# Issuing the two matmuls of a k tile in turn instead of in pairs of two

## The chip, the cores and the metric

The kernel runs on one core of a Trainium2 chip. The metric is the device time of one execution in microseconds (us).

## The reference, cut to what matters

One layer of a hybrid encoder on 256 tokens of width 2048 in f32: a norm, an input projection to a Mamba-2 scan and to a sliding-window attention, an output projection with a residual, and then a retrieval of single-neuron experts (PEER). The change lies in the first product of that retrieval. In the reference it is a gather:

```python
def block(args):
    xb, ib, gb = args
    u = jnp.take(u_tab, ib, axis=0)
    act = jax.nn.gelu(jnp.einsum("thkd,td->thk", u, xb), approximate=False)
    v = jnp.take(v_tab, ib, axis=0)
    return jnp.einsum("thk,thkd->td", gb * act, v)
```

`u_tab` and `v_tab` hold 16384 experts of 2048 numbers; each token picks 128 of them (8 heads, 16 each).

## The kernel before

The kernel doesn't gather from `u_tab`. It computes the product of all 16384 rows with all 256 tokens densely, in 128 chunks of 128 experts (chunks `C_U` to `C_U + 127`), and later uses the values that the routing asks for. Then comes the dense product with `v_tab`.

**The split of a product.** TensorE multiplies numbers rounded to a shorter mantissa (`float32r`). To keep f32 accuracy, weights and activations are both cut into a high and a low part, and a product is high x high + high x low + low x high. For a chunk the raw weights come by DMA into `raw` (four slots of 1024 columns, two per chunk), ScalarE rounds them into `high`, VectorE writes the difference into `low`; `lo_done` counts the halves that are ready, `used` those that TensorE has finished with. The activations lie in `acts`, for each k tile first the 256 columns of the high part, then the 256 of the low part: `hi_tile(k)` is the first, `lo_tile(k)` the second, `both_tiles(k)` the 512 columns of both.

**An ordinary product** (`product`, input projection, output projection and queries) has 16 k tiles, and for each of them three matmuls of 256 columns into one accumulator: high weights x high part, high weights x low part, low weights x high part.

**A product of the expert stage** (`paired=True`, the 128 chunks of `u_tab`) has two matmuls for each k tile. The wide one multiplies the high weights by the 512 columns of both parts into a whole PSUM bank, `ps[:, par, :]`. The narrow one multiplies the low weights by the 256 columns of the high part into the first half of the same bank, `ps[:, par, 0:T]`. Each matmul is preceded by a load of its 128 x 128 weights. ScalarE copies the second half of the bank to SBUF (L865), VectorE adds the first half to it (L1481), ScalarE applies Gelu (L870, L874). Two banks alternate. `paired_product` issues these matmuls: for each two k tiles first the two wide ones (L1739), then the two narrow ones (L1743). It waits for `lo_done` ahead of each half chunk, and in the first chunk for a few counts of `tile_lo` (the dictionary `READY_AT`), while the activations are still being cut.

**The rest of the expert work.** The chunks are issued by a hardware loop of two chunks per turn. Beside them VectorE works out the routing, GpSimd scatters the gates, and SyncE issues the loads. After the last chunk TensorE goes on with `v_tab` (`expert_rows`), where all matmuls are 512 columns wide and successive ones write different PSUM banks (L2102, L2104, L2114, L2116, L2118); its first matmul waits for the weights that VectorE writes from the last product (L1647).

Of the kernel before, what the change touches and what calls it, by code (L numbers as in the profile page):

```python
# [22 lines left out]
P = 128  # L23
T = 256
D = 2048
KT = D // P
# [33 lines left out]
PIECE = 1024  # L60
# [49 lines left out]
def build(nc, x_t, small, id_iota, w_in, w_out, w_q, keys, u_tab, v_tab, g_f, out):  # L110
# [8 lines left out]
    with ExitStack() as ctx:  # L119
        def sb(stack, name, cols, dt=F32):  # L120
            return stack.enter_context(nc.sbuf_tensor(name, [P, cols], dt))

        def sem(name):
            return ctx.enter_context(nc.semaphore(name))

        raw = sb(ctx, "raw", RING * PIECE)
        high = sb(ctx, "high", RING * PIECE, F32R)
        low = sb(ctx, "low", RING * PIECE, F32R)
# [32 lines left out]
        ps = ctx.enter_context(nc.psum_tensor("ps", [P, 8, 512], F32))  # L161
# [90 lines left out]
        hi_tile = lambda k: acts[:, ds(2 * T * k, T)]  # L252
        lo_tile = lambda k: acts[:, ds(2 * T * k + T, T)]
        both_tiles = lambda k: acts[:, ds(2 * T * k, 2 * T)]
# [44 lines left out]
        lo_done = sem("lo_done")  # L299
        used = sem("used")  # L300
# [9 lines left out]
        tile_lo = sem("tile_lo")  # L310
# [1411 lines left out]
        def _(pe):  # L1722
            mm = nc.tensor.matmul

            READY_AT = {0: 8, 8: 14, 14: 15, 15: 16}

            def paired_product(c, par, acc, ready):

                both = ps[:, par, :]
                tile_of = lambda t, s, k: t[:, s * PIECE + k * P:s * PIECE + (k + 1) * P]  # L1730
                for half in range(2):
                    s = 2 * par + half
                    pe.wait_ge(lo_done, 2 * c + half + 1)
                    for two in range(0, 8, 2):
                        for k in (two, two + 1):
                            kk = 8 * half + k
                            if ready is not None and kk in READY_AT:
                                pe.wait_ge(tile_lo, ready + READY_AT[kk])
                            mm(both, tile_of(high, s, k), both_tiles(kk), start=(kk == 0), stop=False,  # L1739
                               skip_group_check=True)  # L1740
                        for k in (two, two + 1):
                            kk = 8 * half + k
                            ins = mm(acc, tile_of(low, s, k), hi_tile(kk), start=False, stop=(kk == KT - 1),  # L1743
                                     skip_group_check=True)
                    ins.then_inc(used, 1)

            def product(c, par, midway=None, ins_hi=None, ins_lo=None, ready=None, late=None,
                        paired=False):

                early = isinstance(c, int) and c in early_bank  # L1750
                if not early:
                    pe.wait_ge(taken, c - 1)
                acc = ps[:, early_bank[c] if early else par, 0:T]
                src_hi, src_lo = (hi_tile, lo_tile) if ins_hi is None else (ins_hi, ins_lo)
                if paired:
                    paired_product(c, par, acc, ready)
                    return
                for half in range(2):
                    s = 2 * par + half
                    pe.wait_ge(lo_done, 2 * c + half + 1)  # L1760
                    for k in range(8):
                        kk = 8 * half + k
                        if ready is not None and kk in READY_AT:
                            pe.wait_ge(tile_lo, ready + READY_AT[kk])
                        if kk == KT - 2 and late:
                            late()
                        a_hi, a_lo = src_hi(kk), src_lo(kk)
                        wh = high[:, s * PIECE + k * P:s * PIECE + (k + 1) * P]
                        wl = low[:, s * PIECE + k * P:s * PIECE + (k + 1) * P]
                        mm(acc, wh, a_hi, start=(kk == 0), stop=False)  # L1770
                        mm(acc, wh, a_lo, start=False, stop=False)  # L1771
                        ins = mm(acc, wl, a_hi, start=False, stop=(kk == KT - 1))  # L1772
                    ins.then_inc(used, 1)
                    if midway and half == 0:
                        midway()
# [86 lines left out]
            first_half(0, 1)  # L1862
            first_half(1, 1)
            product(2, 0)
            product(3, 1, sum_x)
            product(4, 0)
            turn_dt()
            product(5, 1)
# [108 lines left out]
            for s in range(SSD_TILES - 1):  # L1977
                c = C_Q + 1 + s
                acc = ps[:, c % 2, 0:T]
# [95 lines left out]
            for k in range(KT):  # L2075
                ins = nc.tensor.transpose(ps[0:SPARSE, 4 + k // 4, k % 4 * P:(k % 4 + 1) * P],
                                          h_sb[:, k * T + DENSE:(k + 1) * T], ident)
# [18 lines left out]
            def narrow_rows(par, hf, start=False, stop=False):  # L2096

                vh, vl = table_piece(par, hf)
                w = w_t[par]
                acc = [ps[:, 4 + 2 * hf + n, :] for n in range(2)]  # L2100
                for n in range(2):
                    mm(acc[n], w[:, DENSE:DENSE + 2 * SPARSE], vh[n], start=start, stop=False, skip_group_check=True)  # L2102
                for n in range(2):
                    ins = mm(acc[n], w[:, DENSE:DENSE + 2 * SPARSE], vl[n], start=False, stop=stop, skip_group_check=True)  # L2104
                return ins
# [64 lines left out]
            for hf in range(2):  # L2170
                pe.wait_ge(lo_done, 2 * (C_END - 2) + hf + 1)
                ins = narrow_rows(before, hf)
# [88 lines left out]
```

## Time and profile before

| | |
|---|---|
| median of 3 runs | 1730.2 us (1730.1 to 1730.77) |
| the profiled execution | 1730.2 us, span 1728.4 us |
| mean granted TensorE clock | 0.997 of full speed |
| TensorE busy | 1712.3 us, 99% of the span |
| weight loads busy | 1507.2 us, 87% |
| VectorE busy | 1326.5 us, 77% |
| ScalarE busy | 920.3 us, 53% |
| stage of the change | 416.7 to 1130.6 us |

The span runs from the first to the last instruction on the core; the execution's own time adds what lies around it. PE is TensorE's matmuls, PEld its weight loads, DVE is VectorE, ACT ScalarE, POOL GpSimd, SP SyncE. Durations of matmuls overlap, since they are pipelined and their ends are modelled: how fast TensorE works is seen in the distances of the starts.

### The profile page before, as it was taken

Reading aid. Unit: us, or ns where it says so; the run is one execution under the profiler, and the core shown is the slowest. Engines: PE = TensorE matmul, PEld = TensorE weight load, DVE = VectorE, ACT = ScalarE, POOL = GpSimd, SP = SyncE. Lnnn points to the kernel's source line nnn. Section 1 sums busy time; section 2 is a strip of 40 time slices with the busy share of each in tenths; the row PEclk is TensorE's granted clock in tenths of the full one; section 3 lists DMA queues with packets and bytes.
Section 4 is the critical chain, followed back from the end, with each engine's and each line's share of the span. In section 5 each row is a group of like instructions: output and inputs, shape, how many; then the busy total and the mean of one; then the engine's idle time right before and its main releaser. Section 6 shows DMA issues by size and latency. Waiting matters only on the chain.

```text
span 1728.4 us, 27916 instructions
## 1 busy us (share of the span) xinstructions
PE 1712.3 (99%) x10171; PEld 1507.2 (87%) x10171; DVE 1326.5 (77%) x2178; ACT 920.3 (53%) x1567; POOL 542.7 (31%) x336
## 2 busy tenths in 40 slices
PE   9999999999999999999999999999999999999997
PEld 8999999999888888888888888888888888888885
DVE  7878878767999999555555666668878888888887
ACT  6545655444554555544444444455555555555556
POOL 0000000000007787877783000058545422222210
PEclk9999999999999999999999999999999999999999
DMA  7654568776657888877787888898999999999994
GB/s 259 217 195 163 172 190 278 225 237 207 202 192 194 191 194 202 199 190 199 196 192 203 265 264 266 263 365 334 361 342 362 360 360 354 366 363 358 367 333 139
DMA packets 186549, 445.79 MB, mean 258 GB/s; under 512 B 59360, under 2 KB 94448, under 8 KB 177904
## 3 DMA queue, kind: packets, MB, share of 16 engines
q1 hardware_dynamic: 146976, 373.47, 64.1%
q0 software_dynamic: 39504, 71.55, 15.6%
q8 instruction: 25, 0.41, 0.1%
q14 instruction: 44, 0.36, 0.1%
HBM read 423.79 MB, written 20.57 MB: 257 GB/s over the span
## 4 chain that ended last, share of the span: by engine, by line
PE 99%; DMA 0%; DVE 0%; ACT 0%; DVEq 0%; SPq 0%; issue 0%
PE ps L1739 28%; PE ps L1743 14%; PE ps L2118 7%; PE ps L2114 7%; PE ps L2116 7%; PE ps L2102 7%; PE ps L2104 7%; PE ps L1770 4%; PE ps L1771 4%; PE ps L1772 4%; PE ps L1953 3%; PE ps L1954 3%; PE ps L1955 3%; PE ps L2067 0%; DMA raw<-w_in 0%; PE ps L1941 0%
## 5 line engine op out<-in xcount | busy, mean ns | idle before, releaser
L1739 PE MATMUL ps<-acts,high 128*128 128x512 f32 x2048 | 643.5, 395 | 0.0
L960 DVE TENSOR_TENSOR low<-raw,high 128x1024 fp32r<-128x1024 f32 x378 | 460.2, 1222 | 87.3 <-ACT high L644 78.1
L1743 PEld LDWEIGHTS ps<-acts,low 128*128 128x128 f32 x2048 | 384.7, 188 | 91.0
L644 ACT ACTIVATE high<-raw 128x1024 fp32r<-128x1024 f32 x378 | 395.3, 1051 | 85.8 <-PE ps L1772 37.8
L1743 PE MATMUL ps<-acts,low 128*128 128x256 f32 x2048 | 402.3, 278 | 0.0
L1739 PEld LDWEIGHTS ps<-acts,high 128*128 128x128 f32 x2048 | 311.7, 189 | 0.3 <-DVE low L960 0.2
L637 ACT ACTIVATE high<-raw 128x1024 fp32r<-128x1024 f32 x172 | 182.6, 1062 | 171.4 <-PE ps L2118 169.5
L598 POOL DMA_INDIRECT big<-v_tab,half_sb x64 | 119.5, 1868 | 480.1 <-DVE big L1641 287.0
L967 DVE TENSOR_TENSOR low<-raw,high 128x1024 fp32r<-128x1024 f32 x172 | 206.4, 1221 | 64.6 <-ACT high L637 64.4
L578 POOL DMA_INDIRECT gate_scratch<-gates_sb,cells_sb x128 | 208.3, 1627 | 69.5 <-issue 69.5
L865 ACT ACTIVATE side<-ps 128x256 f32<-128x256 f32 x128 | 49.2, 384 | 285.9 <-PE ps L1743 285.9
L1481 DVE TENSOR_TENSOR side<-ps,side 128x256 f32<-128x256 f32 x128 | 53.9, 421 | 136.6 <-ACT side L865 136.6
L1641 DVE SCALAR_TENSOR_TENSOR big<-big,share_sb 128x2048 f32<-128x2048 f32 x64 | 150.1, 2345 | 0.3
L585 POOL DMA_DIRECT2D half_sb<-swap_sb x4 | 4.4, 1110 | 439.9 <-DVE swap_sb L1574 439.9
L637 ACT ACTIVATE high<-raw_more 128x1024 fp32r<-128x1024 f32 x84 | 89.2, 1062 | 81.8 <-PE ps L2118 80.6
L967 DVE TENSOR_TENSOR low<-raw_more,high 128x1024 fp32r<-128x1024 f32 x84 | 100.7, 1221 | 28.5 <-ACT high L637 28.4
L578 POOL DMA_INDIRECT gate_scratch<-half_sb x64 | 107.2, 1674 | 19.5 <-issue 19.5
L606 POOL DMA_INDIRECT share_sb<-act_scratch,cell_ix x64 | 99.7, 1558 | 36.1 <-issue 19.2
L1770 PE MATMUL ps<-acts,high 128*128 128x256 f32 x352 | 101.0, 287 | 0.0
L1771 PE MATMUL ps<-acts,high 128*128 128x256 f32 x352 | 99.5, 283 | 0.0
L1772 PE MATMUL ps<-acts,low 128*128 128x256 f32 x352 | 99.5, 283 | 0.0
L870 ACT ACTIVATE big<-side 128x192 f32<-128x192 f32 x128 | 46.0, 359 | 66.4 <-DVE side L1481 66.3
(286 smaller groups left out, 3202.9 us busy)
## 6 DMA issues: line engine op xcount, KB each, us to landing
raw<-u_tab SPq DMA_DIRECT2D x256, 512.0 KB, 4.3
raw<-v_tab SPq DMA_DIRECT2D x172, 512.0 KB, 7.5
raw_more<-v_tab SPq DMA_DIRECT2D x84, 512.0 KB, 7.4
raw<-w_in SPq DMA_DIRECT2D x62, 512.0 KB, 4.2
raw<-w_out SPq DMA_DIRECT2D x32, 512.0 KB, 4.9
raw<-w_q SPq DMA_DIRECT2D x32, 512.0 KB, 4.9
gate_scratch<-side SPq DMA_DIRECT2D x32, 384.0 KB, 5.7
big<-gate_scratch SPq DMA_DIRECT2D x16, 768.0 KB, 7.5
```

The source lines that it names most:

```text
L578: nc.gpsimd.indirect_dma_start(out=gate_cells, out_offset=bass.IndirectOffsetOnAxis(ap=ix, axis=0), in_=v, in_offset=None, compute_op=ALU. ...
L637: nc.scalar.activation(slot(high, s), v_raw[q % V_RING], ACT.Copy).then_inc(hi_done, 1)
L644: nc.scalar.activation(slot(high, s), slot(raw, s), ACT.Copy).then_inc(hi_done, 1)
L960: V.tensor_tensor(slot(low, s), slot(raw, s), slot(high, s).bitcast(F32), ALU.subtract).then_inc(lo_done, 1)
L967: V.tensor_tensor(slot(low, s), v_raw[q % V_RING], slot(high, s).bitcast(F32), ALU.subtract).then_inc(lo_done, 1)
L1641: V.scalar_tensor_tensor(out=acc_s, in0=row_in[n % ROWS], scalar=share_sb[:, n:n + 1], in1=acc_s, op0=ALU.mult, op1=ALU.add).then_inc(row_ ...
L1739: mm(both, tile_of(high, s, k), both_tiles(kk), start=(kk == 0), stop=False, skip_group_check=True)
L1743: ins = mm(acc, tile_of(low, s, k), hi_tile(kk), start=False, stop=(kk == KT - 1), skip_group_check=True)
L1770: mm(acc, wh, a_hi, start=(kk == 0), stop=False)
L1771: mm(acc, wh, a_lo, start=False, stop=False)
L1772: ins = mm(acc, wl, a_hi, start=False, stop=(kk == KT - 1))
L2102: mm(acc[n], w[:, DENSE:DENSE + 2 * SPARSE], vh[n], start=start, stop=False, skip_group_check=True)
```

## The change

The function `paired_product` and its call are removed. The ordinary loop of `product` gets a branch: with `paired` it issues the wide matmul of a k tile, and then the narrow one of the same k tile. The order of a chunk is then wide 0, narrow 0, wide 1, narrow 1 and so on instead of wide 0, wide 1, narrow 0, narrow 1. Operands, banks, waits per half and the semaphore that the last narrow matmul of a half raises are the same. The flag `stop` of the last wide matmul is now true.

```diff
-            def paired_product(c, par, acc, ready):
-                both = ps[:, par, :]
...
-                    for two in range(0, 8, 2):
-                        for k in (two, two + 1):
...
-                            mm(both, tile_of(high, s, k), both_tiles(kk), start=(kk == 0), stop=False,
-                               skip_group_check=True)
-                        for k in (two, two + 1):
-                            kk = 8 * half + k
-                            ins = mm(acc, tile_of(low, s, k), hi_tile(kk), start=False, stop=(kk == KT - 1),
-                                     skip_group_check=True)
-                    ins.then_inc(used, 1)
...
-                if paired:
-                    paired_product(c, par, acc, ready)
-                    return
...
-                        mm(acc, wh, a_hi, start=(kk == 0), stop=False)
-                        mm(acc, wh, a_lo, start=False, stop=False)
-                        ins = mm(acc, wl, a_hi, start=False, stop=(kk == KT - 1))
+                        if paired:
+                            mm(ps[:, par, :], wh, both_tiles(kk), start=(kk == 0), stop=(kk == KT - 1),
+                               skip_group_check=True)
+                        else:
+                            mm(acc, wh, a_hi, start=(kk == 0), stop=False)
+                            mm(acc, wh, a_lo, start=False, stop=False)
+                        ins = mm(acc, wl, a_hi, start=False, stop=(kk == KT - 1), skip_group_check=paired)
```

## Rows read from the trace of the kernel before

**Rows 1.** The page: the span, TensorE's busy time, granted clock in 40 slices.
```profile
span 1728.4 us, 27916 instructions
...
PE 1712.3 (99%) x10171; PEld 1507.2 (87%) x10171; DVE 1326.5 (77%) x2178; ACT 920.3 (53%) x1567; POOL 542.7 (31%) x336
...
PEclk9999999999999999999999999999999999999999
```

**Rows 2.** The page: the chain that ended last, by engine and by line.
```profile
PE 99%; DMA 0%; DVE 0%; ACT 0%; DVEq 0%; SPq 0%; issue 0%
PE ps L1739 28%; PE ps L1743 14%; PE ps L2118 7%; PE ps L2114 7%; PE ps L2116 7%; PE ps L2102 7%; PE ps L2104 7%; PE ps L1770 4%; PE ps L1771 4%; PE ps L1772 4%; PE ps L1953 3%; PE ps L1954 3%; PE ps L1955 3%; PE ps L2067 0%; DMA raw<-w_in 0%; PE ps L1941 0%
```

**Rows 3.** The page's groups: count, then busy us, mean ns, idle us before.
```profile
L1739 PE MATMUL ps<-acts,high 128*128 128x512 f32 x2048 | 643.5, 395 | 0.0
...
L1743 PEld LDWEIGHTS ps<-acts,low 128*128 128x128 f32 x2048 | 384.7, 188 | 91.0
...
L1743 PE MATMUL ps<-acts,low 128*128 128x256 f32 x2048 | 402.3, 278 | 0.0
L1739 PEld LDWEIGHTS ps<-acts,high 128*128 128x128 f32 x2048 | 311.7, 189 | 0.3 <-DVE low L960 0.2
```

**Rows 4.** Timeline of TensorE (start us, us): first and last wide group of 1024.
```profile
416.72 0.70 PE L1739 MATMUL ps<-acts,high 128*128 128x512 f32 x2
...
1129.90 0.62 PE L1739 MATMUL ps<-acts,high 128*128 128x512 f32 x2
```

**Rows 5.** Timeline of TensorE from 700 us, matmuls, merged in twos.
```profile
700.05 0.63 PE L1739 MATMUL ps<-acts,high 128*128 128x512 f32 x2
700.52 0.39 PE L1743 MATMUL ps<-acts,low 128*128 128x256 f32 x2
700.75 0.62 PE L1739 MATMUL ps<-acts,high 128*128 128x512 f32 x2
701.21 0.40 PE L1743 MATMUL ps<-acts,low 128*128 128x256 f32 x2
701.45 0.63 PE L1739 MATMUL ps<-acts,high 128*128 128x512 f32 x2
701.92 0.39 PE L1743 MATMUL ps<-acts,low 128*128 128x256 f32 x2
702.14 0.63 PE L1739 MATMUL ps<-acts,high 128*128 128x512 f32 x2
```

**Rows 6.** Timeline of the weight loads at the same place.
```profile
700.29 0.42 PEld L1743 LDWEIGHTS ps<-acts,low 128*128 128x128 f32 x2
700.64 0.30 PEld L1739 LDWEIGHTS ps<-acts,high 128*128 128x128 f32 x2
```

**Rows 7.** Timeline of TensorE from 300 us, output projection, nine steps apart.
```profile
299.89 0.28 PE L1953 MATMUL ps<-act_hi,high 128*128 128x256 f32 x1
...
300.97 0.28 PE L1953 MATMUL ps<-act_hi,high 128*128 128x256 f32 x1
```

**Rows 8.** Busy us (and count) by window, granted clock, DMA share, GB/s.
```profile
417.00:700.00 283.00, 282.96 (x1624) 246.68 (x1623) 265.35 (x854) 152.72 (x265) 144.08 (x88) 1.00 0.73 192
1300.00:1700.00 400.00, 400.00 (x1766) 331.24 (x1765) 343.59 (x321) 224.35 (x357) 110.80 (x63) 1.00 0.95 354
```
The columns are the length, then PE, PEld, DVE, ACT and POOL.

**Rows 9.** Timeline of TensorE at 1277 us: transposes with 128 columns each.
```profile
1277.18 3.66 PE L2148 MATMUL ps<-consts,h_back 128*64 128x128 f32 x32
```

**Rows 10.** Waits from 417 to 1130 us: total, times, longest.
```profile
ACT side L865 <- PE ps L1743: 284.5, 123, 3.3
```

**Rows 11.** The chain in order of time, from the last product on.
```profile
1130.79 0.39 ACT side L865
...
1131.21 0.42 DVE side L1481
1131.63 0.28 DVE w_even L1647
```

More of the change, by code:

```diff
@@ L1725, in _ @@
             READY_AT = {0: 8, 8: 14, 14: 15, 15: 16}
-            def paired_product(c, par, acc, ready):
-                both = ps[:, par, :]
[L1730 to L1733, printed above, removed]
-                    for two in range(0, 8, 2):
-                        for k in (two, two + 1):
-                            kk = 8 * half + k
-                            if ready is not None and kk in READY_AT:
-                                pe.wait_ge(tile_lo, ready + READY_AT[kk])
-                            mm(both, tile_of(high, s, k), both_tiles(kk), start=(kk == 0), stop=False,
-                               skip_group_check=True)
-                        for k in (two, two + 1):
-                            kk = 8 * half + k
-                            ins = mm(acc, tile_of(low, s, k), hi_tile(kk), start=False, stop=(kk == KT - 1),
-                                     skip_group_check=True)
-                    ins.then_inc(used, 1)
             def product(c, par, midway=None, ins_hi=None, ins_lo=None, ready=None, late=None,
```

## The prediction

> **What bounds the kernel now.** I read the page's first two parts for who is busy, then the chain, then the timeline of TensorE alone, since the edit is only an order of matmuls. The span is 1728.4 us and the profiled execution took 1730.2 us, 1.8 us more lying around the span; that is also the median of the runs shown, so no correction is needed between the two. TensorE is busy 99% of the span and its granted clock reads 9 tenths or more in every slice, which is the 2.4 GHz level [rows 1]. The chain that ended last runs 99% through TensorE, 28% and 14% of the span on the two lines of the function that goes away [rows 2]. So whatever one matmul of this stage costs more or less reaches the end of the kernel, one for one, as long as nothing else is late.
>
> A busy TensorE is not the answer, because its durations overlap: the 2048 wide matmuls are given 395 ns each and the 2048 narrow ones 278 ns [rows 3], which would sum to 1378 us in a stage of 714 us. What counts is the step from one start to the next. I took it in three ways.
>
> First, the whole stage. The first group of two wide matmuls starts at 416.72 us, the last at 1129.90 [rows 4]; 1024 groups, so 1023 steps: 713.18 / 1023 = 697.1 ns for two k tiles, 348.6 ns for one (one wide and one narrow matmul).
>
> Second, by role. In the three turns from 700.05 to 702.14 us [rows 5] a wide group starts 0.47, 0.46 and 0.47 us ahead of its narrow group, 466.7 ns on average, so 233 ns for a wide matmul. What is left of 697.1 is 230.4 ns for two narrow ones: 115.2 ns each. The weight loads [rows 6] split the groups, since a load starts with the matmul before the one it serves: the group of two L1743 loads begins at 700.29, with the second wide matmul, the group of two L1739 loads at 700.64, with the second narrow one. So the steps of a turn are 700.05 to 700.29 (wide to wide, 0.24), to 700.52 (wide to narrow, 0.23), to 700.64 (narrow to narrow, 0.12), to 700.75 (narrow to wide, 0.11). Within the rounding no place in the turn is dear.
>
> Third, the same widths elsewhere. Where all matmuls are 256 wide, nine of them start in 299.89 to 300.97 us: 120.0 ns each [rows 7]. Where all are 512 wide, 1766 start in 400 us: 226.5 ns each [rows 8]. Streaming at 2.4 GHz is 106.7 and 213.3 ns, so each carries some 13 ns on top there; in the stage of the change the wide one carries 20 and the narrow one 8.5. The sum of the pure steps is 346.5 ns against 348.6 measured.
>
> **The change, part by part.** The removed function issued, for each two k tiles, wide, wide, narrow, narrow. The new branch issues wide, narrow, wide, narrow. Both have 2048 wide and 2048 narrow matmuls with the same operands, banks and widths, each with its own weight load of 128 columns. Nothing is added on ScalarE, VectorE, GpSimd or the DMA queues.
>
> *Streaming.* 2048 x (512 + 256) columns before and after: no change.
>
> *Weight loads.* This is where an order of wide and narrow could matter: a load that starts with a narrow matmul has only some 115 ns of cover. The trace shows loads of 188 to 189 ns [rows 3], yet a narrow matmul is followed after 0.11 to 0.12 us by the next one, whatever its width, so the recorded duration is not what must be covered. What must be is at most some 114 ns, by the row where 32 transposes of 128 columns each with a load of its own take 3.66 / 32 = 114 ns per step at most (the last one runs out within it) [rows 9]; they are of plain f32, so that is the nearest row and not the same one. In the old turn the loads under narrow matmuls are those of the second narrow and of the first wide: two in four. In the new turn all loads of wide matmuls lie under a narrow one and none of the narrow ones': again two in four, 2048 of 4096 in either case. The first wide matmul of the old turn has just such a short-covered load; it follows its predecessor after 0.11 us, and its own step is 0.24 against 0.23 for the second. So the load costs nothing new.
>
> The Trainium skill (page "TensorE: Matmul & The Clock Gate", sections "LDWEIGHTS (loading the stationary operand)" and "Back-to-back issue gap") gives a load of 128 columns as 128/1.2 = 107 ns and the warm gap of a matmul as N/2.4 + 2.5, that is 109 and 216 ns; by it every load is just hidden in both orders and the change is worth 0, but the stage would take 2048 x 325 = 665 us where the trace shows 713, so its gaps are too short for this kernel.
>
> *Steps between matmuls.* The new turn has only the two transitions wide to narrow and narrow to wide. If the step belongs to the matmul and its follower, the new turn takes the old steps wide to narrow (0.23) and narrow to wide (0.11); if to the matmul and its predecessor, the step of a wide one behind a narrow one (0.24) and of a narrow one behind a wide one (0.12). The two readings average 0.35 us, the old 348.6 ns, and their spread of 10 ns to either side is that of rows rounded to 10 ns; the group averages, 233.3 and 115.2, are sharper and sum to 348.5. That is -0.1 ns, times 2048: -0.2 us. I take 0.
>
> For the bounds I take the combinations of the rows that the old order does not yield. The wide one keeps its 233.3 and the narrow one, never again beside its own kind, takes the 120.0 of [rows 7]: 353.3 ns, +4.7 x 2048 = +9.6 us. Or both take the pure steps, 226.5 + 120.0 = 346.5: -2.1 x 2048 = -4.2 us; with the narrow step kept at 115.2 as well, 341.7: -14.1 us. I keep the middle because it alone is measured in a mixture of widths.
>
> *Waits and semaphores.* The wait on the low halves stands ahead of each half chunk in both versions, and the slots are released by the same last narrow matmul of the half. The three waits on the activation tiles bite in the first chunk only; one of them moves behind one narrow matmul, at most 0.2 us and covered. The only stall inside the stage that ends on another engine is 0.2 us on the first load [rows 3], so VectorE, at 265.35 us busy of the first 283, 94%, does not hold TensorE now [rows 8]; ScalarE waits 284.5 us for the products [rows 10]. If TensorE were 1% faster, the 280 us left would still hold VectorE's 265, so a gain would not be eaten there. The stage's last narrow matmuls are the last two instructions before and the last one after; the tail of 0.39, 0.42 and 0.28 us through ScalarE and VectorE to the first expert row [rows 11] hangs on the same last matmul.
>
> Sum: 0 + 0 + 0, on 1730.2 us.
>
> **The rivals.** *A, it becomes slower: the alternation of widths costs what the grouping saved.* Place: the narrow matmul between two wide ones. For it: two narrow ones in a row step 115.2 ns here while narrow ones in threes step 120.0, so something in the grouping does shorten the narrow step, and breaking the group may undo it. Against it: the wide ones pay 7 ns more in the same stage, and the narrow one ahead of a wide one is no dearer than that ahead of a narrow one. Price 1730.2 + 9.6 = 1739.8 us; it decides from 1.7 ns per k tile (3.5 us / 2048) on.
>
> *B, it becomes faster: the even turn reaches the pure steps.* Two matmuls of unlike width then average 346.5 ns. For it: the pure stages do reach it, and 348.6 shows that the grouped order pays 2 ns over it. Against it: nothing in the trace shows a mixture at that rate, and the expert stage changes its PSUM bank with every matmul, which this one does not. Price 1730.2 - 4.2 = 1726.0, in the extreme 1716.1.
>
> *C, the load is exposed.* If a wide matmul had to wait for the whole recorded load of 188 ns under a narrow one of 115, each k tile would cost 73 ns more, +149 us and 1879.7. The old order has the same pairing once in four matmuls at 0.11 to 0.12 us, which all but excludes it.
>
> **How the numbers follow.** The step shown in either role leaves the time as it is: chance 0.51, alone 1728.5 to 1732.0. A has 0.28, since the short narrow step is a feature of the grouping alone; B 0.19, since it asks for something no mixed row shows; C 0.02. A measurement of this kernel tells a change of about 0.2%, 3.5 us, from none. A lies wholly on the slower side if it reaches a third of its price, and B's nearest price lies only 0.7 us beyond the bound, but its extreme far beyond. So faster 0.19, same 0.51, slower 0.30. The range takes in B's near price with a little for the rounding of the steps and all of A: 1725.5 to 1740.5, leaving out B's extreme and C.
>
> **What would show it.** In the profile after, the wide and narrow lines should each count 2048, and the timeline of TensorE should show single matmuls in turn, a wide one starting 0.23 us ahead of the narrow one and that one 0.115 us ahead of the next wide; 16 k tiles would take 5.58 us. A step of 0.12 behind the narrow at 0.23 behind the wide is A; 0.227 and 0.12 is B. The stage must begin at 416.7 us as now, and the expert stage keep its 226.5 ns. What makes the prediction wrong is a dependence of the step on the order itself, on the widths of both neighbours or on the PSUM addresses that two successive matmuls share, which no row of the old order separates.

## The result and the profile after

The changed kernel takes 1740.11 us (median of 5, 1739.69 to 1740.2) against 1730.41 us (median of 5): 9.7 us slower by the medians; the ratio on record is 1.0052, 95% interval 1.0039 to 1.0066. The record lists one more execution of the changed kernel, outside that median, of 1736.79 us; it comes up again below. The forecast of no change was wrong. The time lies in the range given, 0.4 us below its upper end, and near that of rival A, 1739.8 us.

The page of the changed kernel: span, chain by engine and line, and the groups of the two matmuls. L1748 is the wide one, L1753 the narrow one; L1753 now also issues the low product of the ordinary products (L1772 before), so its group holds 352 of these too:

```profile
span 1738.3 us, 27916 instructions
...
PE 97%; DMA 1%; DVE 1%; ACT 0%; SPq 0%; issue 0%; DVEq 0%
PE ps L1748 28%; PE ps L1753 18%; PE ps L2099 7%; PE ps L2095 7%; PE ps L2097 7%; PE ps L2083 7%; PE ps L2085 7%; PE ps L1751 4%; PE ps L1752 4%; PE ps L1934 3%; PE ps L1935 3%; PE ps L1936 3%; DMA big<-x_t 1%; PE ps L2048 0%; DMA raw<-w_in 0%; PE ps L1922 0%
...
L1748 PE MATMUL ps<-acts,high 128*128 128x512 f32 x2048 | 723.8, 399 | 0.0
L1753 PE MATMUL ps<-acts,low 128*128 128x256 f32 x2400 | 674.7, 281 | 0.0
```

The number of instructions is the same to the last one. The path is still TensorE, with 97% of the chain where it had 99%. The span grew by 9.9 us. The narrow line's 18% is not a rise over the 14% of [rows 2]: there L1772 had 4% of its own, and the wide line has 28% in both. The chain doesn't show the loss; the distances of the starts do.

The timeline of TensorE in the changed kernel (start us, us), from the second wide matmul to the seam of the first two chunks, at 700 us, at the end of the stage:

```profile
417.21 0.40 PE L1748 MATMUL ps<-acts,high 128*128 128x512 f32 x1
...
422.07 0.40 PE L1748 MATMUL ps<-acts,high 128*128 128x512 f32 x1
422.30 0.28 PE L1753 MATMUL ps<-acts,low 128*128 128x256 f32 x1
422.44 0.48 PE L1748 MATMUL ps<-acts,high 128*128 128x512 f32 x1
422.76 0.28 PE L1753 MATMUL ps<-acts,low 128*128 128x256 f32 x1
422.88 0.40 PE L1748 MATMUL ps<-acts,high 128*128 128x512 f32 x1
...
699.88 0.40 PE L1748 MATMUL ps<-acts,high 128*128 128x512 f32 x1
700.12 0.28 PE L1753 MATMUL ps<-acts,low 128*128 128x256 f32 x1
700.23 0.40 PE L1748 MATMUL ps<-acts,high 128*128 128x512 f32 x1
700.48 0.28 PE L1753 MATMUL ps<-acts,low 128*128 128x256 f32 x1
700.60 0.40 PE L1748 MATMUL ps<-acts,high 128*128 128x512 f32 x1
700.83 0.28 PE L1753 MATMUL ps<-acts,low 128*128 128x256 f32 x1
700.94 0.40 PE L1748 MATMUL ps<-acts,high 128*128 128x512 f32 x1
...
1140.13 0.40 PE L1748 MATMUL ps<-acts,high 128*128 128x512 f32 x1
```

From the 18th wide matmul at 422.88 us to the last at 1140.13 are 2030 steps: 353.3 ns for a k tile, against 348.6 before. That is 4.7 ns, times 2048 9.6 us: the loss, and all of it in this stage. The reader is to see a second thing in the middle rows. The wide steps are not equal: 0.24, 0.25, 0.23 us, with narrow ones of 0.11, 0.12, 0.11 between them, 1.06 us for three k tiles, and then it begins again. The whole nanoseconds of the trace give 349, 350 and 361 ns for the three k tiles; over the slow stretch the step from a wide matmul averages 236.4 ns and that from a narrow one 117.0. Rival A added up 233.3 and 120.0: only the sum is there.

The stage behind it, the product with `v_tab`, kept its pace: 1767 matmuls in the window 1300 to 1700 us, where [rows 8] has 1766.

### The profile page after: what moved, and what is told of

The parts are those of the page before. It is cut to its first block, busy times and chain, and to the rows that moved or that the text cites. A ratio compares the mean times of both kernels' runs of the same rounds, so it can differ in the third digit from the quotient of the medians.

```text
span 1738.3 us, 27916 instructions
## 1 busy us (share of the span) xinstructions
PE 1722.1 (99%) x10171; PEld 1511.5 (87%) x10171; DVE 1327.9 (76%) x2178; ACT 919.7 (53%) x1567; POOL 544.6 (31%) x336
## 4 chain that ended last, share of the span: by engine, by line
PE 97%; DMA 1%; DVE 1%; ACT 0%; SPq 0%; issue 0%; DVEq 0%
PE ps L1748 28%; PE ps L1753 18%; PE ps L2099 7%; PE ps L2095 7%; PE ps L2097 7%; PE ps L2083 7%; PE ps L2085 7%; PE ps L1751 4%; PE ps L1752 4%; PE ps L1934 3%; PE ps L1935 3%; PE ps L1936 3%; DMA big<-x_t 1%; PE ps L2048 0%; DMA raw<-w_in 0%; PE ps L1922 0%
## 5 line engine op out<-in xcount | busy, mean ns | idle before, releaser
L1748 PE MATMUL ps<-acts,high 128*128 128x512 f32 x2048 | 723.8, 399 | 0.0
L1753 PE MATMUL ps<-acts,low 128*128 128x256 f32 x2400 | 674.7, 281 | 0.0
L1748 PEld LDWEIGHTS ps<-acts,high 128*128 128x128 f32 x2048 | 384.8, 188 | 96.1 <-issue 0.2
L1753 PEld LDWEIGHTS ps<-acts,low 128*128 128x128 f32 x2400 | 454.3, 189 | 0.0
L2083 PE MATMUL ps<-high,w_even 128*128 128x512 f32 x256 | 79.0, 390 | 1.2 <-DVE w_even L1647 1.2
L2085 PE MATMUL ps<-low,w_even 128*128 128x512 f32 x256 | 78.8, 389 | 0.0
```

The costliest lines, as they stand in the source:

```text
L1748: mm(ps[:, par, :], wh, both_tiles(kk), start=(kk == 0), stop=(kk == KT - 1), skip_group_check=True)
L1753: ins = mm(acc, wl, a_hi, start=False, stop=(kk == KT - 1), skip_group_check=paired)
```

## The experiments

The first theories: W, the widths of neighbours fix the step (a change of width costs). R, the narrow matmul pays for rereading what the wide one of its own k tile has just read. P, two matmuls in a row on the same PSUM columns hold each other up. L, the load under the narrow matmul is too long for it. S, pairs are a special rhythm.

**Mirrored pairs.** An edit of the kernel before:

```diff
-                        for k in (two, two + 1):
...
-                        for k in (two, two + 1):
+                        for wide, k in ((True, two), (False, two), (False, two + 1), (True, two + 1)):
```

> For each two k tiles the order is wide 0, narrow 0, narrow 1, wide 1. Widths: again two of each in a row, so two changes of width for four matmuls as in the kernel before; but each turn has one narrow matmul straight behind the wide one of the same k tile, as in the changed kernel. If what counts is the pattern of widths (theory W: a change of width costs, or a wide matmul whose weights load under a narrow one), 697 ns for two k tiles and 1730.2 us. If what counts is that a narrow matmul follows the wide one of its own k tile and rereads its activations (theory R), half of the slow-down stays: about 702 ns and 1735 us.

Measured 1730.56 us, ratio to the kernel before 0.9998 (0.9989 to 1.0007). As many narrow matmuls follow the wide one of their own k tile as do not, and nothing changed: R has no support here, and the sequence of widths, not which k tile they serve, carries the difference.

**Groups of four and of eight.** The same loop with longer groups:

```diff
-                    for two in range(0, 8, 2):
-                        for k in (two, two + 1):
+                    for two in range(0, 8, 4):
+                        for k in range(two, two + 4):
```

(8 in place of 4 in the second kernel.)

> Four wide matmuls, then four narrow ones: one change of width in four matmuls. The pure steps sum to 346.7 ns for a k tile (226.7 + 120.0); pairs of two pay 1.8 ns over that, single alternation 6.7. Theory W by the number of changes (0.5 and 1 per matmul so far, now 0.25): at most 0.9 ns over, 347.6, so 1728.2 us, or 1728.5 if it is not linear. If instead pairs are a special rhythm (theory S) and the longer group falls back to pure steps with one dear seam, anything from 346.7 to 350 ns, 1726.5 to 1733 us.

> Eight wide matmuls, then eight narrow ones, one half chunk. Theory W: 0.4 ns over the pure sum, 347.1 ns for a k tile, 1727.2 us. Theory S: the same rhythm as a group of four, whatever that is. In either case the wide step inside a group should read 226.7 and the narrow one 120.0 as in the pure stages, if the neighbours' width is all that matters.

Groups of four took 1735.3 us, ratio 1.0027 (1.0016 to 1.0039); groups of eight 1731.58 us, ratio 1.0007 (0.9998 to 1.0016). TensorE's timeline with groups of four, the first and last wide group of 512:

```profile
416.86 1.18 PE L1739 MATMUL ps<-acts,high 128*128 128x512 f32 x4
...
1134.08 1.09 PE L1739 MATMUL ps<-acts,high 128*128 128x512 f32 x4
```

and with groups of eight, the first and last narrow group of 256:

```profile
418.68 1.12 PE L1743 MATMUL ps<-acts,low 128*128 128x256 f32 x8
...
1131.04 1.11 PE L1743 MATMUL ps<-acts,low 128*128 128x256 f32 x8
```

717.22 us in 511 steps of four k tiles are 350.9 ns for a k tile; 712.36 in 255 steps of eight are 349.2. As times, groups of four are clearly slower than pairs, and groups of eight can't be told from them. So the order of pace is pairs 348.6, eights 349.2, fours 350.9, single alternation 353.3. Theory W, by which fewer changes of width are cheaper, has fallen: fours have half the changes of pairs and are 4.8 us slower. I had given fours at most 1733 us under any theory; that was a miss too.

**The narrow matmul in another PSUM bank.** On the changed kernel, with the low product left out of the result:

```diff
-                        ins = mm(acc, wl, a_hi, start=False, ...)
+                        ins = mm(ps[:, 6 + par, 0:T] if paired else acc, wl, a_hi, start=(paired and kk == 0), ...)
```

> The changed kernel (single alternation), but the narrow matmuls write a PSUM bank of their own (6 or 7), whose contents nobody reads: the product low weights x high activations is left out of the result. Theory P (two successive matmuls adding to the same PSUM columns hold each other up): the step of a k tile falls from 353.3 to 346.7 ns and the time to 1726.5 us. Theories W and R: unchanged, 353.3 ns and 1740.1 us.

Measured 1737.35 us, ratio 1.0035 (1.0023 to 1.0047): between the two expectations. (Of its ten executions one took 1869.7 us with a mean granted clock of 0.849, where all others in the record have 0.996 to 0.998; it says nothing of the kernel, and the median of the nine others is 1737.22. One took 1728.29 us, the other eight 1736.9 to 1740.2.) The windows of TensorE alone tell why (length, busy us with the count of matmuls that touch the window, granted clock, DMA share, GB/s):

```profile
430.00:580.00 150.00, 150.00 (x867) 1.00 0.68 196
660.00:720.00 60.00, 60.00 (x341) 1.00 0.84 198
800.00:1100.00 300.00, 300.00 (x1700) 1.00 0.78 226
```

867 in 150 us are 346.0 ns for two matmuls, 1700 in 300 us are 352.9. (The count takes in those that run over the edge, so these read about 0.5 ns short; by the starts, the two paces are 346.7 and 353.3.) The same instructions ran at one pace first and at another later. The place of the change, in the timeline of the same kernel:

```profile
588.47 0.39 PE L1748 MATMUL ps<-acts,high 128*128 128x512 f32 x1
588.70 0.28 PE L1753 MATMUL ps<-acts,low 128*128 128x256 f32 x1
589.17 0.50 PE L1748 MATMUL ps<-acts,high 128*128 128x512 f32 x1 [0.19 <-DVE low L960]
589.51 0.28 PE L1753 MATMUL ps<-acts,low 128*128 128x256 f32 x1
```

One wait for VectorE, 0.47 us from start to start where 0.12 is usual, lies between the two paces. As the slow pace of 353.3 ns is there with separate banks as well, P does not explain it. And it sent me back to the changed kernel: its first chunk, too, ran at 0.347 us for a k tile (14 steps from 417.21 to 422.07 us), and the slow pace begins behind the irregular step at 422.44 us.

**Shorter loads.** On the changed kernel, once for the wide matmul and once for the narrow one, 64 of 128 weight columns; half the output rows of the products concerned are left out.

```diff
+                            n = P if kk == 0 else P // 2
-                            mm(ps[:, par, :], wh, both_tiles(kk), ...)
+                            mm(ps[0:n, par, :], wh[:, 0:n], both_tiles(kk), ...)
```

> The changed kernel, but from the second k tile on the wide matmul uses 64 of its 128 weight columns and writes 64 PSUM partitions: its load, which lies under the narrow matmul, is shorter. The high products of half the experts are left out for 15 of 16 k tiles. Theory L (the load under the narrow matmul is too long for its 107 ns of streaming and costs the 6.7 ns over the pure steps): the step of a k tile falls to 346.7 ns or lower, 1726.5 us. Theory W (widths alone): 353.3 ns, 1740.1 us.

> The changed kernel, but the narrow matmul uses 64 of its 128 weight columns: the load under the wide matmul is shorter. The product low weights x high activations is left out for half the experts. This load has 233 ns of cover, so theories L and W both say no change, 353.3 ns and 1740.1 us; a fall here as large as in the run with the wide one's load cut would mean that it is the size of the array used, not the cover, that counts.

With the wide one's load cut 1720.24 us, ratio 0.9939 (0.9923 to 0.9956); with the narrow one's 1723.96 us, ratio 0.9959 (0.9941 to 0.9976), a median between two heaps of five executions each, at 1718.8 to 1719.6 and at 1728.3 to 1728.6. Both fell, so it is not the cover of the one load under the narrow matmul (theory L as I had put it). Windows of TensorE with the wide one's load cut:

```profile
430.00:500.00 70.00, 70.00 (x412) 1.00 0.63 203
800.00:1100.00 300.00, 300.00 (x1733) 1.00 0.80 232
```

346.2 ns late in the stage, the pure sum, and 339.8 early on, under the pure sum, between short waits for VectorE; by the starts, 346.7 and 340.0. The run with the narrow one's load cut has the lower pace too, in a short stretch (first and last of 15 wide matmuls):

```profile
639.72 0.39 PE L1748 MATMUL ps<-acts,high 128*128 128x512 f32 x1
...
644.48 0.39 PE L1748 MATMUL ps<-acts,high 128*128 128x512 f32 x1
```

That is 4.76 us in 14 steps, 340.0 ns. For most of the stage it keeps 346.7. So these kernels have two paces as well, 6.7 ns apart like those of the full matmuls. It is not shown whether the cut takes the slow rhythm away and adds a third one, or makes each of the two 6.7 ns shorter. Of either kernel one execution was profiled, at 1728.4 us, and both ran at 346.7 from 663 us to the end of the stage, 1342 steps. At 340.0 these would be 1342 x 6.7 ns = 9.0 us shorter: 1719.4 us, where the other four of the one lie at 1719.8 to 1720.3 and the lower heap of the other at 1718.8 to 1719.6. That those kept the lower pace is an inference; none of them was profiled. The cut also uses less of the array, and with it the load and the matmul change together; which of the two shortens the pace is not separated.

**Other activations for the narrow matmul.** On the changed kernel; the low product is computed with the wrong activations.

```diff
-                        ins = mm(acc, wl, a_hi, ...)
+                        ins = mm(acc, wl, hi_tile(max(kk - 1, 0)) if paired else a_hi, ...)
```

> The changed kernel, but the narrow matmul reads the high activations of the k tile before (the first one its own) in place of its own: the low product is computed with the wrong activations. Theory R (rereading the columns that the wide one has just read costs): the step falls from 353.3 towards 348.5 ns, 1730 to 1733 us. Theories W and L: 353.3 ns, 1740.1 us.

Measured 1740.05 us, ratio 1.0055 (1.0038 to 1.0072). R is refuted here directly.

**One extra matmul.** What was left is theory K: single alternation has several steady rhythms, and the phase in which it starts selects one. On the changed kernel, once, behind the second chunk, with n = 64, 128, 192:

```diff
             product(C_U + 1, (C_U + 1) % 2, paired=True)
+            mm(ps[:, 7, 0:64], acts[:, 0:P], acts[:, 0:64], start=True, stop=True)
             with pe.Fori(1, N_KEYS // 2) as i:
```

> The changed kernel with one more matmul, 64 columns wide, once behind the second chunk, into a PSUM bank that nobody reads. Theory K (alternation has more than one steady rhythm, 353.3 and 346.7 ns for a k tile, both seen in the runs so far, and the phase in which it is entered selects one until the next stall): the stage sits in one of the two for long stretches, in no third value, and the time is either about 1740.2 us or towards 1727 to 1730. Theory O (the step is fixed by the order and the operands, and the fast stretches seen had another cause): 353.3 ns throughout, 1740.2 us.

> The same with 128 columns. Theory K: one of the two rhythms; of the three widths tried at least one should land in 346.7 ns behind the extra matmul, if a single irregular step is all it takes. Theory O: 353.3 ns, 1740.2 us.

> The same with 192 columns. Theory K: one of the two rhythms, as for the other widths. Theory O: 353.3 ns, 1740.2 us.

64 columns: 1737.46 us, ratio 1.0044 (1.0029 to 1.0058), four of the five executions at 1737.2 to 1737.5 and one at 1740.0. 128 columns: 1740.07 us, ratio 1.0056 (1.0039 to 1.0073). 192 columns: 1740.2 us, ratio 1.0057 (1.004 to 1.0073). TensorE's timeline in the run with 64 columns; L2069 is the extra matmul:

```profile
417.19 0.39 PE L1748 MATMUL ps<-acts,high 128*128 128x512 f32 x1
...
427.78 0.40 PE L1748 MATMUL ps<-acts,high 128*128 128x512 f32 x1
428.02 0.28 PE L1753 MATMUL ps<-acts,low 128*128 128x256 f32 x1
428.13 0.20 PE L2069 MATMUL ps<-acts 128*128 128x64 f32 x1
428.16 0.47 PE L1748 MATMUL ps<-acts,high 128*128 128x512 f32 x1
...
429.29 0.39 PE L1748 MATMUL ps<-acts,high 128*128 128x512 f32 x1
429.52 0.28 PE L1753 MATMUL ps<-acts,low 128*128 128x256 f32 x1
429.64 0.39 PE L1748 MATMUL ps<-acts,high 128*128 128x512 f32 x1
429.87 0.28 PE L1753 MATMUL ps<-acts,low 128*128 128x256 f32 x1
...
594.50 0.40 PE L1748 MATMUL ps<-acts,high 128*128 128x512 f32 x1
...
594.85 0.44 PE L1748 MATMUL ps<-acts,high 128*128 128x512 f32 x1
595.12 0.28 PE L1753 MATMUL ps<-acts,low 128*128 128x256 f32 x1
595.24 0.40 PE L1748 MATMUL ps<-acts,high 128*128 128x512 f32 x1
```

and its windows:

```profile
430.00:580.00 150.00, 150.00 (x868) 1.00 0.68 196
660.00:720.00 60.00, 60.00 (x342) 1.00 0.85 198
800.00:1100.00 300.00, 300.00 (x1699) 1.00 0.78 225
```

Behind the extra matmul the wide steps are all 0.23 and the narrow ones 0.12: 345.6 ns by the first window, 353.1 by the last. The fast pace went on through an irregular step at 589.19 us and ended with a second one at 594.85, 166.7 us or 30 chunks later: 30 x 16 x 6.6 ns = 3.2 us off 1740.1 is 1736.9, and 1737.46 was measured. The two other widths left the stage in the slow rhythm. The changed kernel's execution of 1736.79 us has the time of such a course without any extra matmul; it was not profiled.

The first rows show one thing more. Up to the extra matmul this is the changed kernel, and yet its first chunks ran in the slow rhythm: (427.78 - 417.19) / 30 = 353.0 ns, where the changed kernel's first chunk has 347. So the same instructions with the same operands start in one rhythm in one execution and in the other in another, and the instructions alone don't decide it.

**The extra matmul in the kernel before.** The same line with 128 columns:

> The kernel before (pairs of two) with the extra matmul of 128 columns at the same place. In all its executions so far the pairs took 696.5 to 697 ns for two k tiles, behind stalls too, so theory K says that pairs have one rhythm: unchanged, 348.3 ns for a k tile and 1730.5 us. If pairs too can be moved into another rhythm, the step changes behind the extra matmul, and the advantage of pairs is that they were entered well.

Measured 1730.35 us, ratio 1.0 (0.999 to 1.0009). Pairs kept their pace behind this matmul, 348.3 ns (348.6 is the mean of the whole stage), as behind the irregular steps at 656 to 658 us in their traces. Only one width was tried.

**Two and three extra matmuls.** 64 columns each, behind chunks 2 and 36, and behind 2, 36 and 56, with the loop split there:

```diff
+            mm(ps[:, 7, 0:64], acts[:, 0:P], acts[:, 0:64], start=True, stop=True)
-            with pe.Fori(1, N_KEYS // 2) as i:
+            with pe.Fori(1, 18) as i:
                 for j in range(2):
                     product(C_U + 2 * i + j, (C_U + j) % 2, paired=True)
+            mm(ps[:, 7, 0:64], acts[:, 0:P], acts[:, 0:64], start=True, stop=True)
+            with pe.Fori(18, N_KEYS // 2) as i:
...
```

> The changed kernel with the extra matmul of 64 columns behind chunk 2 and again behind chunk 36, past the two short waits for VectorE (at 589 and 595 us) after which the run with one extra matmul fell back to 353.3 ns for a k tile. Theory K: 346.7 ns up to 589 us, 353.3 to chunk 36, 346.7 from there to the end of the stage if the second one lands as the first did: 94 + 30 chunks of 128 at 16 x 6.6 ns less, so 13 us off 1740.1, plus what VectorE holds back: 1727 to 1729 us, faster than both kernels. Theory K with an unlucky landing: 1737.4 us as with one. Theory O': the extra matmul helps only in the first part of the stage, whatever its phase: 1737.4 us too, but with no step of 346.7 behind chunk 36.

> The same with a third one behind chunk 56. If the rhythm is 353.3 there, it has another chance to move to 346.7 for the last 72 chunks (7.6 us less); if it is already 346.7, the irregular step can throw it back, and then this run is slower than the one with two by up to 7.6 us. Theory K expects each stretch between two irregular steps to keep one of the two values.

With two 1737.07 us, ratio 1.0027 (1.0017 to 1.0038); with three 1730.11 us, ratio 1.0003 (0.9994 to 1.0012). Each kernel's 12 executions fell in two heaps with nothing between: with two, 4 at 1729.7 to 1730.4 us and 8 at 1736.7 to 1737.5; with three, 10 at 1729.1 to 1730.6 and 2 at 1736.8 and 1737.3. None reached the 1727 to 1729 us that I had given for two fast landings. The profiled execution of the one with two took 1730.4 us. Its windows:

```profile
430.00:580.00 150.00, 150.00 (x851) 1.00 0.68 193
660.00:720.00 60.00, 60.00 (x349) 1.00 0.84 199
800.00:1100.00 300.00, 300.00 (x1733) 1.00 0.80 231
```

and its timeline: two wide matmuls ahead of the first extra one, 14 steps apart, then the second wide one behind the second extra one, and the last of the stage:

```profile
422.87 0.40 PE L1748 MATMUL ps<-acts,high 128*128 128x512 f32 x1
...
427.72 0.40 PE L1748 MATMUL ps<-acts,high 128*128 128x512 f32 x1
...
620.85 0.40 PE L1748 MATMUL ps<-acts,high 128*128 128x512 f32 x1
...
1130.45 0.39 PE L1748 MATMUL ps<-acts,high 128*128 128x512 f32 x1
```

Here the second chunk had been fast (427.72 - 422.87 = 4.85 us, 346.4 ns for a k tile), the first extra matmul put the stage into the slow rhythm (851 in 150 us, 352.5 ns), and the second brought the fast one for the rest: (1130.45 - 620.85) / 1470 = 346.7 ns. The eight executions at 1736.7 to 1737.5 us have the time of the run with one extra matmul; none of them was profiled. In the profiled execution with three extra ones the early windows were fast (868 in 150 us), a wait of 0.6 us for VectorE at 656 us threw it into the slow one (341 in 60 us), and the third extra matmul brought it back (2079 in 360 us from 740 us on, 346.3 ns). So one irregular step can move alternation either way, and the stage then keeps its rhythm for hundreds of microseconds. None of these versions is a sure gain on the kernel before: with three the ratio is 1.0003 with an interval around 1.

## Why the prediction was wrong

**What held.** TensorE is the path and each nanosecond of a k tile costs 2048. Streaming, the number of loads under narrow matmuls, waits, semaphores and the tail to the expert stage did not move the time: with them as they are, the one stretch with a new pace accounts for the 9.7 us. The method of reading the distances of the starts, not the busy time, gave the result again after the change. The figure of the Trainium skill for the isolated gap of a warm matmul ("TensorE: Matmul & The Clock Gate", section "Back-to-back issue gap", N/2.4 + 2.5 ns, from which 325 ns for a k tile is an estimate) stays short of every steady pace here, 346.7 at best with full weights. What the same section of the Trainium skill says in words, that the spacing is set by the load and the matmul together, is compatible with the two runs in which either load was halved and the pace fell, but they changed load and matmul together and so don't prove it.

**The step that failed** is "Steps between matmuls", where I took 0. I gave each step to the matmul and one neighbour, and took the pace of the new order from averages of the old one. The runs show that the pace isn't a sum of such parts. The same alternating instructions run at 353.3 or at 346.7 ns for a k tile, in one trace; the slow rhythm has a period of three k tiles (1.06 us), which no table of neighbours can give. In place of the 0 the term measured +4.7 ns for a k tile, 9.6 us; entered in the other rhythm it would have been -1.9 ns. The prediction's last sentence named a dependence of the step on the order itself as what would make it wrong; the chance it got, by way of A, was too low for a quantity that no row showed. The equality of the two readings within 10 ns of rounding was no evidence, since the whole dispute was about 5 ns. The averages by role of the old order, 233.3 and 115.2 ns, were right readings; they don't carry over: in the slow rhythm of the new order they are 236.4 and 117.0.

**Rival A** had the right time to 0.3 us, by luck: it put the whole loss on the narrow step (115.2 to 120.0) and left the wide one at 233.3, and the trace has most of it on the wide one (236.4) and less on the narrow one (117.0). That 233.3 + 120.0 is the measured 353.3 is, as far as the runs show, a coincidence or a trace of the same unknown cause; A's mechanism is not shown.

**Rival B** exists: alternation does reach 346.7 ns (predicted 346.5), and would give 1740.1 - 2048 x 6.6 ns = 1726.6 us if it lasted. In the profiled execution of the changed kernel only the first chunk has it; the irregular step at the seam at 422.44 us ends it. The execution of 1736.79 us may have kept it until about 595 us. The nearest that an alternation with full weights came is 1728.29 us, the one execution with the separate bank.

**Rival C**, the exposed load at 1879.7 us, was far off, as said. The row that the bound of 114 ns came from was read too simply: by the trace 16 of the 32 transposes have a load of 64 columns, not 128. What I had said of VectorE, that a gain would not be eaten there, was wrong in a way that matters: waits for it came at 589 us in the fast rhythm and at 656 us in another execution, where the kernel before has 94% busy VectorE in that stretch [rows 8]. They cost under 1 us each, but each could end the fast rhythm. The kernel before has an irregular step in that stretch too, at 656 us, and goes on at its old pace.

**What stays open** is why TensorE has these rhythms. Shown is that the slow one is there with separate PSUM banks and with another k tile for the narrow matmul, that the number of changes of width doesn't rank the orders, that the two traces with a weight operand halved have no steady stretch at 353.3 ns, and that pairs kept one pace in all their traces. Why pairs are steady, and whether the load or the columns of the array matter in the halved runs, was not settled.

## What to carry to other kernels

Where TensorE is the path, measure the step from start to start in several stretches of the stage, not one: one order of matmuls can have two steady paces 2% apart, and a mean hides them. An order of unlike matmuls can't be priced from the steps of another order; try it, with more executions than usual, and look for two heaps in their times. A small difference that hangs on the phase in which a loop is entered is also fragile: pairs of two at 348.6 ns are worth more here than an alternation that takes 346.7 or 353.3 as it falls.

## What the hardware showed that I had not expected

- Alternating matmuls of 512 and 256 columns run at 346.7 or 353.3 ns per pair with the same instructions, and one irregular step can switch between them, in either direction: 0.47 us where 0.12 is usual, 0.31 where 0.23 is, or, at the seam behind the first chunk in two of the runs, a k tile that took only 354 or 359 ns. Not each such step does: the one at 589.19 us in the run with 64 columns did not.
- The pace of 346.7 comes in two forms: even k tiles of 346 to 347 ns (the run with 64 columns up to 589 us), and 350 and 343 ns in turn (the first chunk of the changed kernel, and the end of the run with three extra matmuls).
- Longer groups are not monotonic: groups of 1, 2, 4 and 8 took 353.3 (mostly), 348.6, 350.9 and 349.2 ns for a k tile.
- With 64 of 128 weight columns in the wide or in the narrow matmul the pair ran at 340.0 ns in places, under the sum of the pure steps of full matmuls, 346.5. The steady paces of all alternations here, 340.0, 346.7 and 353.3 ns, lie 6.7 ns apart.
